# Down matrices of the middle experts fetched by one transfer of 4 MB into two adjacent slots

## The reference, cut to what matters

```
def _moe(t, w_router, b_router, w_gu, b_gu, w_down, b_down):
    logits = t @ w_router + b_router
    top_val, top_idx = lax.top_k(logits, 4)          # of 32 experts
    top_w = jax.nn.softmax(top_val)
    ...
    hgu  = tok[rows] @ w_gu[e] + b_gu[e]             # w_gu[e]: 1024 x 2048, 8 MB
    gate = jnp.minimum(hgu[:, 0::2], 7.0)
    up   = jnp.clip(hgu[:, 1::2], -7.0, 7.0)
    act  = (up + 1.0) * (gate * jax.nn.sigmoid(1.702 * gate))
    y    = act @ w_down[e] + b_down[e]               # w_down[e]: 1024 x 1024, 4 MB
    out[token] += y * weight
```

## Time and profile before

| | |
|---|---|
| time, median of 3 runs | 1272.92 us (1272.65 to 1280.71) |
| the profiled execution's own time | 1272.74 us |
| its span, first to last instruction | 1270.9 us |
| TensorE busy | 1131.2 us, 89% |
| mean granted TensorE clock | 0.943 |
| DMA rate over the span | 359 GB/s |
| bytes read | 454.15 MB |
| share of the chain that ended last | PE 62%, DMA 31%, SPq 5% |

### The profile page before, as it was taken

The page is one execution under the profiler, slowest core; times in us unless marked ns, Lnnn a source line. Parts: engine busy times, 40 slices in busy tenths (PEclk is TensorE's granted clock), DMA queues, the critical chain, the costliest instruction groups (busy, mean ns, idle before and its releaser), DMA issues.

```text
span 1270.9 us, 19125 instructions
## 1 busy us (share of the span) xinstructions
PE 1131.2 (89%) x7463; PEld 518.3 (41%) x7464; DVE 306.0 (24%) x799; ACT 202.4 (16%) x441; POOL 17.4 (1%) x24
## 2 busy tenths in 40 slices
PE   9999999999999996759976958899798969799886
PEld 4565778888544331213322312133232313233321
DVE  3244443462142220102211201022121102122211
ACT  2116432353021110001110100011010101011100
POOL 1100000000000000000000000000000000000000
PEclk9999999999999997979987988899899889899998
DMA  8943347425589999999999999999999999999997
GB/s 306 343 158 133 112 153 265 155 115 198 211 359 421 426 429 427 428 428 428 428 428 428 429 428 427 429 389 430 428 428 428 428 428 428 428 428 427 429 428 320
DMA packets 58871, 455.64 MB, mean 359 GB/s; under 512 B 7636, under 2 KB 13624, under 8 KB 34136
## 3 DMA queue, kind: packets, MB, share of 16 engines
q1 hardware_dynamic: 58472, 454.55, 86.6%
q10 hardware_dynamic: 304, 0.53, 0.1%
q0 software_dynamic: 64, 0.13, 0.0%
HBM read 454.15 MB, written 1.05 MB: 358 GB/s over the span
## 4 chain that ended last, share of the span: by engine, by line
PE 62%; DMA 31%; SPq 5%; issue 1%; DVE 1%; ACT 0%; ACTq 0%; DVEq 0%
DMA mem<-in_w_gu 30%; PE bank L1151 17%; PE bank L1169 8%; PE bank L613 6%; PE bank L760 6%; PE bank L1069 4%; SPq L396 3%; PE bank L1090 3%; PE bank L1130 2%; PE bank L922 2%; PE bank L668 2%; PE bank L956 2%; PE bank L602 1%; PE bank L944 1%; SPq L526 1%
## 5 line engine op out<-in xcount | busy, mean ns | idle before, releaser
L1151 PE MATMUL bank<-mem 128*32 128x512 f32 x2944 | 384.7, 655 | 129.9 <-DMA mem<-in_w_gu 129.2
L1151 PEld LDWEIGHTS bank<-mem 128*32 128x32 f32 x2944 | 90.6, 116 | 388.6 <-issue 202.2
L1169 PE MATMUL bank<-mem 128*32 128x512 f32 x1456 | 170.5, 597 | 0.0
L1926 DVE TENSOR_SCALAR mem<-bank 128x256 f32<-128x256 f32 x46 | 19.5, 425 | 475.4 <-PE bank L1151 475.4
L1478 ACT ACTIVATE mq<-bank 64x512 f32<-64x512 f32 x46 | 27.1, 590 | 529.8 <-PE bank L1169 526.4
L1069 PEld LDWEIGHTS bank<-mem,sc 128*128 128x128 f32 x768 | 87.6, 192 | 20.9 <-issue 20.9
L1169 PEld LDWEIGHTS bank<-mem 128*32 128x32 f32 x1456 | 42.2, 110 | 121.8 <-issue 121.8
L1069 PE MATMUL bank<-mem,sc 128*128 128x64 f32 x768 | 91.1, 277 | 0.0
L613 PE MATMUL bank<-mem 128*128 128x512 f32 x192 | 83.4, 592 | 0.0
L1090 PE MATMUL bank<-mq,mem 128*128 128x512 f32 x176 | 80.3, 599 | 0.0
L760 PE MATMUL bank<-mem 128*128 128x256 f32 x320 | 71.6, 381 | 0.0
(11 more groups left out here) (313 smaller groups left out, 761.1 us busy)
## 6 DMA issues: line engine op xcount, KB each, us to landing
mem<-in_w_gu SPq DMA_DIRECT2D x128, 2048.0 KB, 40.3
mem<-in_w_down SPq DMA_DIRECT2D x63, 2048.0 KB, 38.8
mem<-in_w_in SPq DMA_DIRECT2D x13, 2048.0 KB, 12.3
mem<-in_w_out SPq DMA_DIRECT2D x2, 2048.0 KB, 8.4
mem<-in_w_mem_kv SPq DMA_DIRECT2D x4, 512.0 KB, 5.5
mem<-in_w_mem_kv SPq DMA_DIRECT2D x1, 2048.0 KB, 10.2
mem<-in_cmp_w_k SPq DMA_DIRECT2D x1, 2048.0 KB, 8.2
mem<-in_cmp_w_v SPq DMA_DIRECT2D x1, 2048.0 KB, 9.4
```

The costliest lines, as they stand in the source:

```text
L1151: mm = nc.tensor.matmul(BH[n][32 * s:32 * s + 32, :], xgT[:, k, 32 * n:32 * n + 32], w[:, c, 512 * s:512 * s + 512], start=k == 0, stop=k ...
L1169: mm = nc.tensor.matmul(BG[64 * hh + 32 * two:64 * hh + 32 * two + 32, :], actT[:, o:o + 32], w[:, r, 512 * hh:512 * hh + 512], start=d == ...
```

## The change

`slot_no` moves the odd seats' q = 3 to slot 10 and their q = 4 to slot 9, which is adjacent to slot 11. For the seats 2 to 30 SP waits once, for the second half's `down_done`, and fetches the whole down matrix by one transfer (`load_down`): 32 KB in each partition, contiguous in memory and in the slots. TensorE waits for that transfer's semaphore before either half. For the seats 0 and 1 and the last one the matrix still comes in halves, with semaphores of their own; for seat 1 the first half of the down matrix is now issued where q = 3 was and q = 3 where the first half was. `last_down` waits for three semaphores at the same rows as before.

```diff
         def slot_no(q, odd):
-            return q if not odd else NSLOT + q if q < 4 else 6 + q
+            return (q, (6, 7, 8, 10, 9, 11)[q])[odd]
...
+        down_full = S("down_full_even"), S("down_full_odd")
+        half_down = S("half_down_even"), S("half_down_odd")
+        def down_rows(e):
+            return w_dn[e].rearrange("(p r) n -> p (r n)", p=P)
+        def load_down(sp, e, odd):
+            a = slots_at[slot_no(4, odd)]
+            sp.dma_start(mem[:, a:a + 2 * SLOT], down_rows(e)).then_inc(down_full[odd], 16)
+        def load_half_down(sp, e, d, odd, sem):
+            sp.dma_start(slot[slot_no(4 + d, odd)], down_rows(e)[:, SLOT * d:SLOT * d + SLOT]).then_inc(sem, 16)
...
-            for q in (5, 0, 1):
-                arrived(sp, ("bgn01", "bgn11", None, None, None, "pl11")[q])
+            arrived(sp, "pl11")
+            load_half_down(sp, 0, 1, 0, half_down[0])
+            for q in (0, 1):
+                arrived(sp, ("bgn01", "bgn11")[q])
                 load_chunk(sp, 0, q, False)
...
-            for q in (3, 4):
-                arrived(sp, f"wo{q - 3}1")
-                load_chunk(sp, 0, q, False)
+            arrived(sp, "wo01")
+            load_chunk(sp, 0, 3, False)
+            arrived(sp, "wo11")
+            load_half_down(sp, 0, 0, 0, down_full[0])
             arrived(sp, "lT")
-            load_chunk(sp, 1, 3, True)
+            load_half_down(sp, 1, 0, 1, half_down[1])
             arrived(sp, "rank")
             sp.wait_ge(S("x2_ready"), 2)
-            load_chunk(sp, 1, 4, True)
+            load_chunk(sp, 1, 3, True)
             sp.wait_ge(S("wts_ready"), 1)
-            load_chunk(sp, 1, 5, True)
+            load_half_down(sp, 1, 1, 1, down_full[1])
...                                         # in load_round
-                for q in (4, 5):
-                    sp.wait_ge(S("down_done"), f * 2 + (q - 3))
-                    if q == 5 and final:
-                        ...                 # two transfers of 1 MB
-                    else:
-                        load_chunk(sp, ahead, q, not odd)
+                if final:
+                    sp.wait_ge(S("down_done"), f * 2 + 1)
+                    load_half_down(sp, ahead, 0, 1, S("last_down0"))
+                    sp.wait_ge(S("down_done"), f * 2 + 2)
+                    for h in range(2):
+                        ...                 # two transfers of 1 MB
+                else:
+                    sp.wait_ge(S("down_done"), f * 2 + 2)
+                    load_down(sp, ahead, not odd)
...                                         # on TensorE
             def down(d, e, odd):
-                w = landed(4 + d, e, odd).rearrange("p (r n) -> p r n", r=4)
+                pe.wait_ge(down_full[odd], e * 8 + (8 if odd else 16))
+                w = slot[slot_no(4 + d, odd)].rearrange("p (r n) -> p r n", r=4)
...
+            for odd in range(2):
+                pe.wait_ge(half_down[odd], 16)
```

More of the change, by code:

```diff
@@ L527, in load_round @@
                                      b_gu[bass.ds(ahead, 1), :].rearrange("o (s n) -> (o s) n", s=4)).then_inc(brow_in[not odd], 16)
-                for q in (4, 5):
-                    sp.wait_ge(S("down_done"), f * 2 + (q - 3))
-                    if q == 5 and final:
[L531 to L534, removed]
-                    else:
-                        load_chunk(sp, ahead, q, not odd)
+                if final:
[3 more added lines that the diff above has]
+                    for h in range(2):
+                        o = SLOT // 2 * h
+                        sp.dma_start(slot[SLOT_ODD_LAST][:, o:o + SLOT // 2],
+                                     down_rows(ahead)[:, SLOT + o:SLOT + o + SLOT // 2]).then_inc(S(f"last_down{1 + h}"), 16)
+                else:
+                    sp.wait_ge(S("down_done"), f * 2 + 2)
+                    load_down(sp, ahead, not odd)
             sp.wait_ge(S("idx_ready"), 1)
@@ L1094, in last_down @@
             def last_down():
[L1096 to L1101, removed]
+                for r in range(8):
+                    if r % 2 == 0 and r != 2:
+                        pe.wait_ge(S(f"last_down{(r - 2) // 2 if r else 0}"), 16)
+                    w = slot[slot_no(4 + r // 4, 1)].rearrange("p (r n) -> p r n", r=4)[:, r % 4]
+                    o, two = 32 * r, r % 2
                     for hh in range(2):
                         mm = nc.tensor.matmul(BG[64 * hh + 32 * two:64 * hh + 32 * two + 32, :], actT[:, o:o + 32],
-                                              w[:, r, 512 * hh:512 * hh + 512], start=False, stop=r >= 2, skip_group_check=True)
-                mm.then_inc(S("down_done"), 1)
+                                              w[:, 512 * hh:512 * hh + 512], start=r < 2, stop=r >= 6, skip_group_check=True)
+                    if r % 4 == 3:
+                        mm.then_inc(S("down_done"), 1)
             def left_scatter():
```

## The result

The changed kernel takes 1275.49 us (median of 18 runs) against 1272.38 us of the kernel before (18 runs). The ratio is 1.0030 with a 95% interval of 1.0017 to 1.0044: slower by about 3.8 us, between 2.2 and 5.6. That is a third of a percent, inside the 1% for which I had 0.95 (and which I had called about the least that can be told from none; the interval is narrower than that) and inside the range, but on the other side of no change than my sum, which came out 0.3 us faster. So the question is where some 4 us against the sum came from.

A forecast was written before the change was run, and what follows sets the result against it. The prediction took one stream of weights with a deep queue, plus a tail, as the bound. 1272.74 - 2.9 + 1.7 + 0.9 = 1272.4, with 0.2 for the median 1272.6 us; range 1269 to 1277.5.

The forecast's parts named there:

- What bounds the kernel: Expert phase: one stream of weights plus a tail, with one gap at 840 to 850 us set by TensorE's chain.
- The wait before the first half: At the four-item expert's first down product TensorE stalls for the whole matrix, delaying its slots' release: +1.7 us.
- third rival: TensorE's pause at 817.8 is followed by a stretch at lower clock, costing 4.3 us: 1276.9 us; chance 0.12.
- The one wait on SP: Merged issue comes 1.7 us later, so the refill of the four-item expert's slots after the gap is late: +0.9 us.
- The rate: Weight stream: 32 KB rows as single packets save 0.10 us per merged matrix, -2.9 us over 29 experts.
- first rival: Rows of 32 KB stay packets of 16 KB, so the stream is not shortened: 1275.5 us; chance 0.18.
- The rule of the fixed part: Every transfer pays about 2 us; if serially, 29 fewer save 67 us: 1206 us; as fourth rival, chance 0.02.
- Things at nothing: Start with seats 0 and 1, their swapped transfers, fewer SP instructions, and the tail: no cost or gain expected.

The follow-up runs named there:

- e1: Changed kernel with only odd seats' slots and seat 1's transfer order kept, halves again fetched, released and waited for singly: 1272.86 us against 1272.04, ratio 1.0001.
- e10: Changed kernel with the down matrices of seats 16 and 18 again in halves, released and waited for singly: 1268.84 us against 1272.34, ratio 0.9968.
- e2: e1 plus TensorE waiting for both halves before reading the first, transfers still 2 MB and issued as before: 1275.90 us, ratio 1.0038 to the kernel before.
- e5: Changed kernel with every down matrix in four 1 MB transfers, issued and waited for together: 1282.32 us, ratio 1.0073 to the kernel before.
- e11: The changed kernel again, unaltered, in a later series: 1276.97 us against 1272.34 of the kernel before, ratio 1.0034.
- e3: e1 plus SP issuing both halves only when the second has been read, TensorE waiting for each singly: 1271.92 us, ratio 0.9992 to the kernel before.
- e6: Changed kernel with both halves of the previous item's down product moved after q2 and bias of the left item: 1270.38 us, ratio 0.9985 to the kernel before.
- e7: Changed kernel with the previous item's down product after the left item's q3, VectorE's activations only after it: 1270.84 us, ratio 0.9987 to the kernel before.
- e8: Kernel before without the transfers of the b_gu rows of seats 2 to 31: 1269.22 us, ratio 0.998.
- e9: Kernel before with only e6's moved order on TensorE, halves handled as before: 1271.79 us against 1272.34, ratio 0.9988.

## Why the prediction was wrong, step by step

**What bounds the kernel: right.** One stream, one gap, and the gap's end set by TensorE's chain from seat 16's q3. Of the waits that the change brings, none outside this stretch and its refill is seen to cost time (e1, e10).

**The wait before the first half: the step that failed.** The prediction put +1.7 us, 819.5 - 817.8, and in its sum nothing for the clock behind the pause. The place was right, and so was the landing of the second half: 9.7 to 9.9 us after q3 in every profile. The hold grew by 4.9 us, 3.2 more than that term (4.7 and 3.0 where TensorE's order is unchanged). Two things were wrong.

The larger one is the clock behind the wait, put at nothing. From `down(0)` to the issue nothing but 29.5 us of matmuls stands in the chain, and in all five profiles with the wait these took 1.6 to 2.8 us longer, 2.3 on average: behind pauses of 2.8 to 4.5 us the two next groups took up to 3.64 and 3.05 us instead of 1.9. That was my third rival's mechanism, held at 0.12; it came every time, at about half of the 4.3 us that I had priced. What I had against it, that TensorE had been busy for 8 us when the pause comes, did not hold it off.

The smaller one is the moment at which TensorE gets to the down product. 817.80 belongs to an execution in which TensorE was at its lower clock from 804.77 to some 815: the group of 48 took 8.22 us, and 5.49 at the upper one (e2). At that clock it arrives 5.5 us after q3 and waits 4.2 to 4.5 (e2, e5, e11). A low clock ahead of the wait had hidden more than half of that stall, and I took the profile's moment for the kernel's. Against what the kernels without the wait do on average the price is less than the stall, 2.4 us for the 1.7 written, since their clock too was low for a part of this group in each profile (6.7 to 8.1 us to the down product). Whether they would ever arrive after 5.5, no profile shows.

**The one wait on SP: right by the trace, +1.1 for the +0.9 written.** The time of e3 alone speaks against it, the landings to the end of the stream for 0.6 to 0.9 us of it. Everywhere else the queue had enough in hand, as read.

**The rate: right in kind, too large.** Rows of 32 KB are single packets, the first rival is out; that its price, 1275.5, is the measured median is a coincidence. But I took 0.10 us for each matrix from one short window of transfers of 1 MB; the merged stretches show 0.10 and 0.07, e5 0.07 to 0.09 for 8 packets. Over 29 matrices that is 2.0 to 2.9 us, where 2.9 stood. The rule of the fixed part, paid serially, is out: 29 fewer transfers gave back 2 to 3 us, what the packets are worth, and not 67, which agrees with the 4.90 us between landings.

**The new sum,** made from the traces after the fact: -2.4 + 4.9 + 1.1 = +3.6 us; measured +3.8 (2.2 to 5.6). With the stall and the refill taken out and 27 matrices merged it would be -2.3; e10 measured -4.1 (-6.1 to -1.9). The 1.8 between them lies within the interval, and where it would be from is open.

**Things at nothing: nothing seen against them.** For the start and the swapped transfers that is e1, within 2 us; in the tail, from the last landing to the end of the span is 8.4 us before and in the changed kernel's first profile.

## What to carry to other kernels

Merging two transfers into one also merges what waits for them: price the consumer's wait for the later half at the one place where the queue runs dry behind it, with what the pause does to the consumer's clock, and leave that place unmerged. When a stall is the difference of two moments, take each at the clock that the engine may have, not at the one of the profile: a slow consumer in one execution hides a wait that a fast one pays. Waits of the same kind where the queue stays full, ten of them with 13.9 us here, may be worth nothing.

## What the runs showed of the hardware beside that

**The tail has several lengths.** In the profiles of e1, e6 and e11 the last item's down product fell into a stretch of low clock. Its group in e1, and in the changed kernel's first profile:

```profile
1263.30 6.09 PE L1118 MATMUL bank<-mem 128*32 128x512 f32 x32
```

```profile
1264.11 3.75 PE L1123 MATMUL bank<-mem 128*32 128x512 f32 x32
```

Together with the scatter ahead of it that adds about 5 us from the last landing to the end of the span: 13.3 or 13.4 in these three against 8.4 in six others (e5, e7, e8 and e9 have 9.5 or 9.6). Each of the three profiled executions is the slowest run of its kernel's series (but so is e3's, with 8.4), so this may be a part of the scatter of single runs here, and it is a reason to compare landings, not ends.

**A late landing that costs nothing.** In five profiles (after, e6, e7, e9, e11) seat 2's q0 landed 6.5 to 7.9 us after the transfer ahead instead of 4.9; in the others it did not. A landing is that of the slowest of 16 DMA engines, and in the changed kernel's profile fifteen of them were done 2.4 us before the last. By seat 16 nothing of it was left: from the issue of seat 2's q0 to the landing of seat 16's q3 it is 435.1 us in the changed kernel, 435.6 in e9 and at most 436.7 (e11) with the late landing, and 436.9 before, 435.9 in e1 and 434.6 in e10 without it. What held that one engine back is open.
